# An earlier second and third operand and a sum made by VectorE in the seven-product matrix multiplication of a transformer block

## The chip, the cores and the metric

The kernel runs on one core of one Trainium2 chip. The time is that of one execution on the device, in microseconds (us), and lower is better. The engines are named as the profile names them: PE is TensorE, which multiplies matrices (PEld is its loading of weights), DVE is VectorE, ACT is ScalarE, POOL is GpSimd, SP is SyncE, which here only issues transfers. DMA transfers are issued by SP, and by POOL where they add to what the destination holds.

## The reference

A block of two attention branches and an MLP is followed by two layers of a second kind. The change touches the MLP of the first block only. With x of 512 tokens by 1024 and D_FF = 4096:

```python
h2 = rms_norm(x, norm_mlp[l])
x = x + jnp.square(jax.nn.relu(h2 @ w_up[l])) @ w_down[l]
```

All arithmetic is in float32. The kernel keeps that precision by splitting each operand into a high part and a low part and by running three passes (high by high, high by low, low by high) over them.

## The kernel before

The MLP is cut into four chunks of 1024 columns of D_FF. In each chunk PE first makes eight tiles of h2 @ w_up (the up products, `up_product`, 24 matmuls each), and then multiplies the squared result (the state) by a 1024 x 1024 block of w_down. In the first three chunks (`FAST` = 3) this second multiplication is done by two-by-two blocks in seven products in place of eight, `fast_product(c, n)` with n from 0 to 6. I call them P0 to P6. Each is 48 matmuls, in two halves b = 0 and 1 that go to two banks. P0 and P1 write tiles named G in the profile, P2, P3 and P6 tiles named T, P4 and P5 tiles named S.

**Weight operands.** Each product has a weight operand of 128 x 2048 elements (1 MB), made of the blocks (row half q, column half p) of w_down in the chunk. They lie in four buffers, called a and c (the two halves of K.raw), f (K.down_f) and e (K.down_e). In the order of the products the buffers are f, a, c, a, c, f, e. A block is loaded by SP (`down_block`), and a second one is added onto it in one of three ways:

- by an adding transfer of 1 MB that POOL issues, line 1138 in `block_added`: P0's operand f (semaphore f_sum), P1's operand a (a_sum), P5's operand f (f_sum again) and P4's operand c (c_sum);
- by DVE, line 1987, which writes e - c into a for P3 (semaphore w_made);
- not at all: P2 takes c and P6 takes e as loaded.

**Splitting.** Each operand then passes through two steps before PE can use it: `down_hi(c, n)`, line 1458, ACT writes the high part into the slab `K.w[:, j % 2]`, and `down_lo(c, n)`, line 1951, DVE writes the low part (raw minus high) and raises w_lo. PE waits for w_lo in `slab_ready`. There are two slabs, so the high part of P1 waits until the eighth up product has ended (tile_full), and that of a later product n until P(n-2) has ended (prod).

**The state.** The eight up tiles come in four pairs i = 0 to 3. For each tile k DVE takes the rectified value (`rectified`, line 1930), ACT squares it into `K.stage` (line 1474, h_sq), POOL makes four combinations of each pair (`state_combined(c, i)`, lines 1128 to 1133, h_comb), and ACT and DVE split the pieces: `state_hi` (line 1434) and `state_lo` (line 1937) for the plain ones, `state_hi_rest` and `state_lo_rest` for one turned piece and three combined ones. P2 is the first product that reads combined pieces of pair 3.

**Results.** `product_in(c, n, b)`, lines 1964 and 1966, adds a finished half of a product into x on DVE.

Each engine executes its own program in the order in which it is written, and a wait holds everything behind it on that engine. Thus the order of `state_combined` and `block_added` on POOL sets when each adding transfer starts, the order in `fast_chunk` of ACT sets when each high part starts, and that of DVE when each low part starts. SP loads block (0, 1) into f as soon as P0's low part is done.

Of the kernel before, what the change touches and what calls it, by code (L numbers as in the profile page):

```python
# [15 lines left out]
ALU = mybir.AluOpType  # L16
# [6 lines left out]
KT = D // P  # L23
# [65 lines left out]
READS = 2 * sum(len(to) for to in LANDS)  # L89
PLAIN_LO, TURNED_LO, MIXED_LO, STATE_LOS = (1, 2, 5, 8), (3, 6, 9, 11), (4, 7, 10, 12), 12  # L90
DOWN_SLABS = tuple(J_MLP + FAST_SLABS * c + HALF + n for c in range(FAST) for n in range(PRODUCTS))
# [101 lines left out]
def allocate(nc, ctx, K):  # L193
# [188 lines left out]
    K.a_sum = semaphore("a_sum")  # L382
    K.c_sum = semaphore("c_sum")
    K.w_made = semaphore("w_made")
# [585 lines left out]
def program_pool(nc, pool, K):  # L970
# [170 lines left out]
    for c in range(FAST):  # L1141
        state_combined(c, 0)
        pool.wait_ge(K.f_in, 64 * c + 32)
        block_added(c, 1, 0, K.down_f[:, :], K.f_sum)
        state_combined(c, 1)
        pool.wait_ge(K.a_in, 32 * (c + 1))
        block_added(c, 1, 1, down_raw(K, c, 1), K.a_sum)
        state_combined(c, 2)
        state_combined(c, 3)
        pool.wait_ge(K.f_in, 64 * (c + 1))  # L1150
        block_added(c, 0, 0, K.down_f[:, :], K.f_sum)
        pool.wait_ge(K.w_lo, down_slab(c, 2) + 1 + QA_MORE)
        pool.wait_ge(K.w_made, c + 1)
        block_added(c, 0, 1, down_raw(K, c, 4), K.c_sum)

# [55 lines left out]
def program_act(nc, act, K):  # L1211
# [231 lines left out]
    def down_hi(c, n):  # L1443


        if n < 2:
            act.wait_ge(K.tile_full, F_MLP + KT * c + 6 + 2 * n)
        else:
            act.wait_ge(K.prod, 2 * (PRODUCTS * c + n - 1))
        if n in (0, 5):  # L1450
            act.wait_ge(K.f_sum, 32 * c + (32 if n else 16))
        elif n in (1, 4):
            act.wait_ge(K.c_sum if n == 4 else K.a_sum, 16 * (c + 1))
        elif n == 3:
            act.wait_ge(K.w_made, c + 1)
        else:
            act.wait_ge(K.c_in if n == 2 else K.e_in, 32 * (c + 1))
        nc.scalar.activation(K.w[:, down_slab(c, n) % 2, 0, :], down_raw(K, c, n), ACT.Copy).then_inc(K.w_hi, 1)  # L1458

    def fast_chunk(c):  # L1460
        f = F_MLP + KT * c
        for i in range(4):
            if i == 0 and c:
                act.wait_ge(K.prod, 2 * PRODUCTS * c)
            if i < 3:
                split(Num(up_slab(c, i + 1)), Num(f + 2 * i))
            else:
                down_hi(c, 0)
            for k in range(2 * i, 2 * i + 2):
                act.wait_ge(K.tile_out, G_MLP + KT * c + k + 1)  # L1470
                if k % 2 == 0 and HALF * c + i >= 2:
# [4 lines left out]
                if k % 2 == 0:  # L1476
                    act.wait_ge(K.h_sq, KT * c + k + 1)
                    state_hi(c, i, B11, B12 + 1)
                    if i:
                        state_hi_rest(c, i - 1)  # L1480
        down_hi(c, 1)
        state_hi_rest(c, 3)
        for n in range(2, PRODUCTS):
            down_hi(c, n)
# [148 lines left out]
def program_vector(nc, dve, K):  # L1633
# [335 lines left out]
    def fast_chunk(c):  # L1969
        for i in range(4):  # L1970
            for k in range(2 * i, 2 * i + 2):
# [3 lines left out]
                if k % 2 == 0:  # L1975
                    state_lo(c, i, B11, B12 + 1, PLAIN_LO[i])
                    if i:
                        state_lo_rest(c, i - 1)
            if i < 2:
                split(Num(up_slab(c, i + 2)))  # L1980
# [7 lines left out]
        product_in(c, 0, 0)  # L1988
        for n in range(1, PRODUCTS):
            if n == 1:  # L1990
                down_lo(c, 2)
                state_lo_rest(c, 3)
            product_in(c, n - 1, 1)
            if 1 < n < PRODUCTS - 1:
                down_lo(c, n + 1)
            if n == PRODUCTS - 1:
                split(Num(up_slab(c + 1, 0)))
            product_in(c, n, 0)
        product_in(c, PRODUCTS - 1, 1)
        split(Num(up_slab(c + 1, 1)))  # L2000
# [836 lines left out]
```

## Time and profile before

| | |
|---|---|
| median of three runs | 1456.66 us (1454.26 to 1458.71) |
| profiled execution | 1456.53 us |
| its span in the trace | 1454.7 us |
| PE busy | 1434.6 us, 99% of the span |
| DVE, ACT, POOL busy | 58%, 44%, 30% |
| mean granted clock of PE | 0.997 of full speed |
| the three chunks with seven products | about 378 to 631 us |

The median lies 0.13 us above the profiled execution, whose time is 1.8 us above its span. A row of the timeline shows the start and the length of an instruction, or of a run of like ones; in brackets stands the time that the engine was idle ahead of it and what ended that. Instructions that issue DMA show the time of the issue only, and the landing has a view of its own. The rows themselves stand in the last section ahead of the prediction.

### The profile page before, as it was taken

What the parts mean: (1) busy time and instruction counts of PE and PEld (TensorE: products, weight loads), DVE (VectorE), ACT (ScalarE), POOL (GpSimd) and SP (SyncE); (2) the same over time, 40 slices, a digit from 0 to 9 for tenths busy, and PEclk for the clock granted to TensorE, in tenths of its full rate; (3) what the DMA queues carried; (4) which work ended last, traced back from release to release, by engine and by line L of the source; (5) the groups of instructions that cost most, each with busy time, mean ns of one, the idle gap of its engine ahead of it and who ended that gap; (6) DMA issues with size and microseconds to landing.
All of it is one profiled execution on the core that took longest, in us unless ns stands there. A gap on an engine that the chain in (4) does not pass through costs nothing.

```text
span 1454.7 us, 19451 instructions
## 1 busy us (share of the span) xinstructions
PE 1434.6 (99%) x7493; PEld 1219.8 (84%) x7493; DVE 841.0 (58%) x1354; ACT 638.6 (44%) x981; POOL 431.8 (30%) x421
## 2 busy tenths in 40 slices
PE   9999999999999999999999999999999999999999
PEld 7888888888888898988888888888888888888887
DVE  5648864444565665754478795444446879543432
ACT  5436862234343434334434695343333469533221
POOL 3004521011330504200406885121120678510000
PEclk9999999999999999999999999999999999999999
DMA  5564332324474675722232123222323212322232
GB/s 197 84 126 115 108 108 92 113 87 148 115 171 146 146 181 145 169 95 87 73 111 71 30 59 113 91 87 91 112 73 110 72 30 59 111 92 87 87 103 71
DMA packets 163788, 151.51 MB, mean 104 GB/s; under 512 B 36136, under 2 KB 141872, under 8 KB 163696
## 3 DMA queue, kind: packets, MB, share of 16 engines
q1 hardware_dynamic: 157200, 137.61, 31.7%
q0 software_dynamic: 6336, 12.58, 5.1%
q8 instruction: 60, 0.98, 0.3%
q14 instruction: 32, 0.26, 0.1%
q10 hardware_dynamic: 160, 0.07, 0.0%
HBM read 139.96 MB, written 2.92 MB: 98 GB/s over the span
## 4 chain that ended last, share of the span: by engine, by line
PE 86%; DVE 5%; ACT 3%; issue 2%; DMA 2%; POOL 2%; DVEq 0%; ACTq 0%; POOLq 0%
PE G L2273 61%; PE G L2255 3%; PE G L2731 3%; PE S L2255 3%; PE T L2364 3%; PE S L2566 2%; DMA raw<-in_w_down 2%; PE G L2388 2%; PE G L2395 2%; PE G L2485 1%; PE T L2566 1%; DVE w L1951 1%; ACT w L1458 1%; DVE sq L1778 1%; ACT w L1223 1%
## 5 line engine op out<-in xcount | busy, mean ns | idle before, releaser
L2273 PE MATMUL G<-gx,w 128*128 128x512 f32 x2928 | 672.3, 390 | 1.3 <-DVE w L1641 1.3
L2273 PEld LDWEIGHTS G<-gx,w 128*128 128x128 f32 x2928 | 548.5, 188 | 116.6 <-DVE w L1641 1.9
L1641 DVE TENSOR_TENSOR w<-raw,w 128x2048 fp32r<-128x2048 f32 (+3 forms) x97 | 221.8, 2286 | 206.5 <-ACT w L1223 206.3
L1223 ACT ACTIVATE w<-raw 128x2048 fp32r<-128x2048 f32 (+2 forms) x99 | 183.0, 1849 | 64.0 <-PE G L2731 14.9
L989 POOL TENSOR_TENSOR t<-t,rden 128x512 f32<-128x512 f32 (+2 forms) x128 | 108.8, 852 | 114.0 <-DVE rden L1784 112.1
L1031 POOL TENSOR_TENSOR t<-sig 128x512 f32<-128x512 f32 x24 | 35.4, 1474 | 338.1 <-DVE sig L1852 338.1
L1285 ACT ACTIVATE t<-sq,nm 128x512 f32<-128x512 f32 (+3 forms) x128 | 80.1, 626 | 17.1 <-DVE nm L1778 16.5
L2273 PE MATMUL G<-kvb,w 128*128 128x512 f32 x384 | 87.4, 389 | 0.0
L2273 PEld LDWEIGHTS G<-kvb,w 128*128 128x128 f32 x384 | 72.1, 188 | 15.0
L1679 DVE SCALAR_TENSOR_TENSOR sig<-G,rstd 128x512 f32<-128x512 f32 x48 | 32.8, 686 | 78.4 <-PE G L2273 78.4
L2364 PE MATMUL T<-ident,t 128*128 128x128 f32 x400 | 66.5, 277 | 3.4 <-POOL t L989 2.4
L1341 ACT ACTIVATE sig<-sig,lp 128x512 f32<-128x512 f32 x32 | 23.2, 724 | 103.0 <-DVE sig L1679 103.0
L2364 PEld LDWEIGHTS T<-ident,t 128*128 128x128 f32 x400 | 47.0, 140 | 22.5 <-POOL t L989 15.6
L2255 PE MATMUL S<-ab 96*128 96x512 f32 x192 | 56.8, 407 | 0.0
L1852 DVE TENSOR_TENSOR sig<-G,sig 128x512 f32<-128x512 f32 x48 | 32.0, 687 | 40.9 <-PE G L2273 40.9
L980 POOL TENSOR_TENSOR sumsq<-sumsq,sq 128x512 f32<-128x512 f32 x21 | 28.6, 1362 | 87.7 <-ACT sq L1241 69.5
L1799 DVE TENSOR_TENSOR pt<-T,pt 128x256 fp32r<-128x256 f32 (+2 forms) x96 | 50.6, 528 | 6.4 <-ACT pt L1329 3.2
L2566 PE MATMUL T<-hc,w 128*128 128x256 f32 x432 | 53.4, 284 | 0.3
L2566 PEld LDWEIGHTS T<-hc,w 128*128 128x128 f32 x432 | 52.3, 192 | 0.7 <-DVE hc L1937 0.7
L1778 DVE CUSTOM_DVE_ANT_0 sq<-S,zeros,hr 128x512 f32<-128x512 f32 x64 | 47.4, 743 | 5.7 <-PE S L2255 4.7
L1128 POOL TENSOR_TENSOR stage<-stage 128x256 f32<-128x256 f32 x12 | 10.0, 834 | 130.7 <-ACT stage L1474 130.7
L1474 ACT ACTIVATE stage<-t 128x512 f32<-128x512 f32 x24 | 15.2, 632 | 75.5 <-DVE t L1930 75.5
(285 smaller groups left out, 2277.6 us busy)
## 6 DMA issues: line engine op xcount, KB each, us to landing
raw<-in_w_in SPq DMA_DIRECT2D x98, 512.0 KB, 7.2
raw<-in_w_up SPq DMA_DIRECT2D x32, 512.0 KB
raw<-in_w_out SPq DMA_DIRECT2D x24, 512.0 KB
raw<-in_w_down SPq DMA_DIRECT2D x20, 512.0 KB, 4.3
down_f<-in_w_down SPq DMA_DIRECT2D x12, 512.0 KB, 5.2
down_f<-in_w_down POOLq DMA_DIRECT2D x6, 1024.0 KB, 10.0
raw<-in_w_down POOLq DMA_DIRECT2D x6, 1024.0 KB, 9.1
raw<-in_w_attn_proj SPq DMA_DIRECT2D x8, 512.0 KB
```

Source lines behind the costliest of these rows:

```text
L989: nc.gpsimd.tensor_tensor(p, p, K.rden[:, n % 4:n % 4 + 1].broadcast_to([P, (hi - lo) * P]), ALU.mult).then_inc(K.probs_ok, 1)
L1031: nc.gpsimd.tensor_tensor(K.t[:, m, :], sig[:, m, :], sig[:, 2 + m, :], ALU.add).then_inc(K.mix_ok, 1)
L1223: nc.scalar.activation(high, cut(K.raw[:, j % 2, 0:n]), ACT.Copy).then_inc(K.w_hi, 1)
L1285: nc.scalar.activation(K.t[:, n % 3, 0:width], K.sq[:, n % 2, 0:width], ACT.Exp, bias=K.nm[:, n % 4:n % 4 + 1], scale=-1.0, accum_out=K.de ...
L1641: nc.vector.tensor_tensor(low, cut(K.raw[:, s, 0:n]), high.bitcast(F32), ALU.subtract).then_inc(K.w_lo, 1)
L1778: nc.vector.tensor_tensor_reduce(K.sq[:, n % 2, c], K.S[(S + n) % 2][:, 0:(b1 - b0) * P], bias, scale, first, ALU.add, ALU.min, K.nm[:, n ...
L1799: nc.vector.tensor_tensor(K.pt[A.at(n)][m % 2][:, 1, b0:b1, e, :], K.T[(U + n) % 2][:, 0:(b1 - b0) * P].rearrange("p (k c) -> p k c", c=P) ...
L2255: mm = nc.tensor.matmul(bank, lhs, rhs, start=(i == 0), stop=(i == len(pairs) - 1))
L2273: mm = nc.tensor.matmul(b[:, :], w(p, k), x(q, k), start=(k == i == 0), stop=(k == kts - 1 and i == len(PASSES) - 1))
L2364: mm = nc.tensor.transpose(K.T[(U + n) % 2][:, k * P:(k + 1) * P], K.t[:, n % 3, c:c + P], K.ident[:, :])
L2566: mm = nc.tensor.matmul(product_bank(K, n, b)[:, m % 2 * SEQ // 2:(m % 2 + 1) * SEQ // 2], w[:, p, k, m * P:(m + 1) * P], K.hc[:, q, k, OP ...
L2731: mm = nc.tensor.matmul(b[:, :], K.m2[:, q, half * HALF + k, t * P:(t + 1) * P], w[:, p, k, :], start=(half == k == p == q == 0), stop=(ha ...
```

## The change

In each of the three chunks:

- ACT makes the high part of P1's operand ahead of the square of the eighth tile, and that of P2's operand right behind this square. The rest of the state parts of pair i - 1 now goes ahead of the squares of pair i, and not behind the first of them. DVE has the matching order, and the counts `PLAIN_LO`, `TURNED_LO` and `MIXED_LO` say after how many parts each is there.
- POOL makes the combinations of pair 2 ahead of the adding transfer of P1's operand, not behind it.
- The adding transfer of P4's operand is gone. DVE adds block (0, 1), which lies in f, onto c (new line 2000 of the changed kernel). As f must keep this block until then, the adding transfer of P5's operand now waits for this sum (w_made at an even count), where it waited for the load of f alone.
- In DVE's program for the products, the second half of a result goes in ahead of the next operand's low part.

POOL's program from the combinations of pair 1 on in chunk 0, before, with the lines of the kernel. The transfer `raw<-in_w_down` is P1's sum:

```order
L1138 DMA down_f<-in_w_down 128x4x512 [waits f_in]
L1128 TENSOR_TENSOR stage<-stage 128x256 [waits h_sq]
L1129 TENSOR_TENSOR stage<-stage 128x256
L1131 TENSOR_TENSOR stage<-stage 128x256 [waits h_comb]
L1133 TENSOR_TENSOR stage<-stage 128x256 [waits h_comb]
L1138 DMA raw<-in_w_down 128x4x512 [waits a_in]
L1128 TENSOR_TENSOR stage<-stage 128x256 [waits h_sq]
L1129 TENSOR_TENSOR stage<-stage 128x256
L1131 TENSOR_TENSOR stage<-stage 128x256 [waits h_comb]
L1133 TENSOR_TENSOR stage<-stage 128x256 [waits h_comb]
```

And now, where each line number is one lower:

```order
L1137 DMA down_f<-in_w_down 128x4x512 [waits f_in]
L1127 TENSOR_TENSOR stage<-stage 128x256 [waits h_sq]
L1128 TENSOR_TENSOR stage<-stage 128x256
L1130 TENSOR_TENSOR stage<-stage 128x256 [waits h_comb]
L1132 TENSOR_TENSOR stage<-stage 128x256 [waits h_comb]
L1127 TENSOR_TENSOR stage<-stage 128x256 [waits h_sq]
L1128 TENSOR_TENSOR stage<-stage 128x256
L1130 TENSOR_TENSOR stage<-stage 128x256 [waits h_comb]
L1132 TENSOR_TENSOR stage<-stage 128x256 [waits h_comb]
L1137 DMA raw<-in_w_down 128x4x512 [waits a_in]
L1127 TENSOR_TENSOR stage<-stage 128x256 [waits h_sq]
L1128 TENSOR_TENSOR stage<-stage 128x256
```

P1's sum moved from ahead of the combinations of pair 2 to behind them, and of the two transfers that followed each other at the end one is left, which waits for w_made.

ACT's program in chunk 1, from the high part of P0 (`w<-down_f`) to that of P6 (`w<-down_e`), before:

```order
L1458 ACTIVATE w<-down_f 128x2048 [waits f_sum,tile_full]
L1474 ACTIVATE stage<-t 128x512 [waits h_lo,tile_out]
L1434 ACTIVATE hc<-stage 128x512 [waits prod,h_sq]
L1434 ACTIVATE hc<-stage 128x256 [waits prod,h_sq]
L1434 ACTIVATE hc<-stage 128x1024 [waits prod,h_comb]
L1474 ACTIVATE stage<-t 128x512 [waits tile_out]
L1458 ACTIVATE w<-raw 128x2048 [waits a_sum,tile_full]
L1434 ACTIVATE hc<-stage 128x256 [waits prod,h_sq]
L1434 ACTIVATE hc<-stage 128x1024 [waits prod,h_comb]
L1458 ACTIVATE w<-raw 128x2048 [waits c_in,prod]
L1458 ACTIVATE w<-raw 128x2048 [waits w_made,prod]
L1458 ACTIVATE w<-raw 128x2048 [waits c_sum,prod]
```

And now, where line 1458 is line 1454 and line 1434 is line 1430:

```order
L1454 ACTIVATE w<-down_f 128x2048 [waits f_sum,tile_full]
L1430 ACTIVATE hc<-stage 128x256 [waits prod,h_sq]
L1430 ACTIVATE hc<-stage 128x1024 [waits prod,h_comb]
L1474 ACTIVATE stage<-t 128x512 [waits h_lo,tile_out]
L1430 ACTIVATE hc<-stage 128x512 [waits prod,h_sq]
L1454 ACTIVATE w<-raw 128x2048 [waits a_sum,tile_full]
L1474 ACTIVATE stage<-t 128x512 [waits tile_out]
L1454 ACTIVATE w<-raw 128x2048 [waits c_in,prod]
L1430 ACTIVATE hc<-stage 128x256 [waits prod,h_sq]
L1430 ACTIVATE hc<-stage 128x1024 [waits prod,h_comb]
L1454 ACTIVATE w<-raw 128x2048 [waits w_made,prod] x2
L1454 ACTIVATE w<-down_f 128x2048 [waits f_sum,prod]
```

The first `w<-raw`, which is P1's high part and waits for a_sum, moved from behind the last square (line 1474) to ahead of it, and P2's (which waits for c_in) from behind the last two state parts to ahead of them.

DVE's program in chunk 1, from the low part of P1, before (1987 makes e - c, 1964 takes a result in):

```order
L1951 TENSOR_TENSOR w<-raw,w 128x2048 [waits w_hi]
L1987 TENSOR_TENSOR raw<-down_e,raw 128x2048 [waits w_lo,c_in,e_in]
L1964 TENSOR_TENSOR x<-G,x 128x2x256 [waits prod_in,prod]
L1951 TENSOR_TENSOR w<-raw,w 128x2048 [waits w_hi]
L1942 SCALAR_TENSOR_TENSOR hc<-stage,hc 128x256 [waits h_hi]
L1937 TENSOR_TENSOR hc<-stage,hc 128x1024 [waits h_hi]
L1964 TENSOR_TENSOR x<-G,x 128x2x256 [waits prod_in,prod] x3
L1951 TENSOR_TENSOR w<-raw,w 128x2048 [waits w_hi]
L1964 TENSOR_TENSOR x<-T,x 128x2x256 [waits prod_in,prod] x2
```

And now, where line 1951 is line 1949, line 1987 line 1985 and line 1964 line 1962:

```order
L1949 TENSOR_TENSOR w<-raw,w 128x2048 [waits w_hi]
L1985 TENSOR_TENSOR raw<-down_e,raw 128x2048 [waits w_lo,c_in,e_in]
L1962 TENSOR_TENSOR x<-G,x 128x2x256 [waits prod_in,prod] x2
L1949 TENSOR_TENSOR w<-raw,w 128x2048 [waits w_hi]
L1940 SCALAR_TENSOR_TENSOR hc<-stage,hc 128x256 [waits h_hi]
L1935 TENSOR_TENSOR hc<-stage,hc 128x1024 [waits h_hi]
L1962 TENSOR_TENSOR x<-G,x 128x2x256 [waits prod_in,prod]
L2000 TENSOR_TENSOR raw<-raw,down_f 128x2048 [waits w_made,w_lo,f_in]
L1962 TENSOR_TENSOR x<-G,x 128x2x256 [waits prod_in,prod]
L1949 TENSOR_TENSOR w<-raw,w 128x2048 [waits w_hi]
```

Between the low parts of P2 and P3 stands the new sum of line 2000, with a result ahead of it and one behind it; one more result moved ahead of P2's low part.

The diff:

```diff
--- before.py
+++ after.py
@@ -87,7 +87,7 @@
 STARTS = (True, True, True, False, True, False, False)
 LANDS = (((1, 0, 1),), ((1, 1, 1),), ((1, 1, 1),), ((0, 1, -1),), ((0, 0, -1),), ((0, 1, 1),), ((1, 0, -1), (0, 0, 1)))
 READS = 2 * sum(len(to) for to in LANDS)
-PLAIN_LO, TURNED_LO, MIXED_LO, STATE_LOS = (1, 2, 5, 8), (3, 6, 9, 11), (4, 7, 10, 12), 12
+PLAIN_LO, TURNED_LO, MIXED_LO, STATE_LOS = (1, 4, 7, 10), (2, 5, 8, 11), (3, 6, 9, 12), 12
 DOWN_SLABS = tuple(J_MLP + FAST_SLABS * c + HALF + n for c in range(FAST) for n in range(PRODUCTS))
 G_LAST = G_L + (LAYERS - 1) * GL + 100
 
@@ -380,7 +380,6 @@
     K.a_in = semaphore("a_in")
     K.f_sum = semaphore("f_sum")
     K.a_sum = semaphore("a_sum")
-    K.c_sum = semaphore("c_sum")
     K.w_made = semaphore("w_made")
     K.prod = semaphore("prod")
     K.prod_in = semaphore("prod_in")
@@ -1143,15 +1142,12 @@
         pool.wait_ge(K.f_in, 64 * c + 32)
         block_added(c, 1, 0, K.down_f[:, :], K.f_sum)
         state_combined(c, 1)
+        state_combined(c, 2)
         pool.wait_ge(K.a_in, 32 * (c + 1))
         block_added(c, 1, 1, down_raw(K, c, 1), K.a_sum)
-        state_combined(c, 2)
         state_combined(c, 3)
-        pool.wait_ge(K.f_in, 64 * (c + 1))
+        pool.wait_ge(K.w_made, 2 * (c + 1))
         block_added(c, 0, 0, K.down_f[:, :], K.f_sum)
-        pool.wait_ge(K.w_lo, down_slab(c, 2) + 1 + QA_MORE)
-        pool.wait_ge(K.w_made, c + 1)
-        block_added(c, 0, 1, down_raw(K, c, 4), K.c_sum)
 
     for k in range(1, KT):
         for i, (total, square) in enumerate(((K.sumsq_f, K.sq_f), (K.sumsq, K.sq))):
@@ -1450,9 +1446,9 @@
         if n in (0, 5):
             act.wait_ge(K.f_sum, 32 * c + (32 if n else 16))
         elif n in (1, 4):
-            act.wait_ge(K.c_sum if n == 4 else K.a_sum, 16 * (c + 1))
+            act.wait_ge(K.w_made if n == 4 else K.a_sum, 2 * (c + 1) if n == 4 else 16 * (c + 1))
         elif n == 3:
-            act.wait_ge(K.w_made, c + 1)
+            act.wait_ge(K.w_made, 2 * c + 1)
         else:
             act.wait_ge(K.c_in if n == 2 else K.e_in, 32 * (c + 1))
         nc.scalar.activation(K.w[:, down_slab(c, n) % 2, 0, :], down_raw(K, c, n), ACT.Copy).then_inc(K.w_hi, 1)
@@ -1466,7 +1462,11 @@
                 split(Num(up_slab(c, i + 1)), Num(f + 2 * i))
             else:
                 down_hi(c, 0)
+            if i:
+                state_hi_rest(c, i - 1)
             for k in range(2 * i, 2 * i + 2):
+                if k == KT - 1:
+                    down_hi(c, 1)
                 act.wait_ge(K.tile_out, G_MLP + KT * c + k + 1)
                 if k % 2 == 0 and HALF * c + i >= 2:
                     act.wait_ge(K.h_lo, STATE_LOS * (c - (i < 2)) + MIXED_LO[(i + 2) % 4])
@@ -1476,11 +1476,9 @@
                 if k % 2 == 0:
                     act.wait_ge(K.h_sq, KT * c + k + 1)
                     state_hi(c, i, B11, B12 + 1)
-                    if i:
-                        state_hi_rest(c, i - 1)
-        down_hi(c, 1)
+        down_hi(c, 2)
         state_hi_rest(c, 3)
-        for n in range(2, PRODUCTS):
+        for n in range(3, PRODUCTS):
             down_hi(c, n)
         act.wait_ge(K.prod, 2 * (PRODUCTS * c + 6))
         split(Num(up_slab(c + 1, 0)), Num(0))
@@ -1973,9 +1971,9 @@
                     dve.wait_ge(K.h_sq, KT * c + k - 2)
                 rectified(k, Num(G_MLP + KT * c + k), Num(F_MLP + KT * c + k))
                 if k % 2 == 0:
-                    state_lo(c, i, B11, B12 + 1, PLAIN_LO[i])
                     if i:
                         state_lo_rest(c, i - 1)
+                    state_lo(c, i, B11, B12 + 1, PLAIN_LO[i])
             if i < 2:
                 split(Num(up_slab(c, i + 2)))
             if i == 2:
@@ -1987,15 +1985,19 @@
         nc.vector.tensor_tensor(down_raw(K, c, 3), K.down_e[:, :], down_raw(K, c, 2), ALU.subtract).then_inc(K.w_made, 1)
         product_in(c, 0, 0)
         for n in range(1, PRODUCTS):
+            product_in(c, n - 1, 1)
+            if n < PRODUCTS - 1:
+                down_lo(c, n + 1)
+            else:
+                split(Num(up_slab(c + 1, 0)))
             if n == 1:
-                down_lo(c, 2)
                 state_lo_rest(c, 3)
-            product_in(c, n - 1, 1)
-            if 1 < n < PRODUCTS - 1:
-                down_lo(c, n + 1)
-            if n == PRODUCTS - 1:
-                split(Num(up_slab(c + 1, 0)))
             product_in(c, n, 0)
+            if n == 1:
+                dve.wait_ge(K.f_in, 64 * (c + 1))
+                dve.wait_ge(K.w_lo, down_slab(c, 2) + 1 + QA_MORE)
+                dve.wait_ge(K.w_made, 2 * c + 1)
+                nc.vector.tensor_tensor(down_raw(K, c, 4), down_raw(K, c, 4), K.down_f[:, :], ALU.add).then_inc(K.w_made, 1)
         product_in(c, PRODUCTS - 1, 1)
         split(Num(up_slab(c + 1, 1)))
 
```

## Rows read from the trace of the kernel before

**Rows 1.** The page, part 1: busy time, share of span, instructions of each engine.

```profile
PE 1434.6 (99%) x7493; PEld 1219.8 (84%) x7493; DVE 841.0 (58%) x1354; ACT 638.6 (44%) x981; POOL 431.8 (30%) x421
```

**Rows 2.** Timeline of PE, chunk 0: start us, us, engine, line, tiles [idle before].

```profile
419.50 7.51 PE L2566 MATMUL G<-hc,w 128*128 128x256 f32 x48 [1.88 <-DVE w L1951]
```

**Rows 3.** Timeline of PE, from 440 us, the products of chunks 1 and 2.

```profile
500.36 12.05 PE L2566 MATMUL G<-hc,w 128*128 128x256 f32 x96
527.03 11.78 PE L2566 MATMUL S<-hc,w 128*128 128x256 f32 x96 [2.66 <-DVE w L1951]
...
587.95 12.05 PE L2566 MATMUL G<-hc,w 128*128 128x256 f32 x96
...
613.22 11.77 PE L2566 MATMUL S<-hc,w 128*128 128x256 f32 x96 [1.25 <-DVE w L1951]
```

**Rows 4.** Timeline of all engines, chunk 0.

```profile
406.02 3.35 DVE L1951 TENSOR_TENSOR w<-down_f,w 128x2048 fp32r<-128x2048 f32 x1 [2.51 <-ACT w L1458]
...
419.58 2.60 DVE L1987 TENSOR_TENSOR raw<-down_e,raw 128x2048 f32<-128x2048 f32 x1
419.98 1.29 POOL L1138 DMA_DIRECT2D down_f<-in_w_down  x1
...
439.43 10.82 PE L2566 MATMUL S<-hc,w 128*128 128x256 f32 x88 [0.91 <-DVE w L1951]
```

**Rows 5.** Timeline of all engines, chunk 1.

```profile
473.74 11.77 SPq L878 DMA_DIRECT2D raw<-in_w_down  x4
474.25 1.29 POOL L1138 DMA_DIRECT2D down_f<-in_w_down  x1
...
490.25 1.29 POOL L1138 DMA_DIRECT2D raw<-in_w_down  x1 [5.05 <-DMA raw<-in_w_down]
490.47 0.63 ACT L1474 ACTIVATE stage<-t 128x512 f32<-128x512 f32 x1 [2.69 <-DVE t L1930]
...
492.95 2.91 DVE L1951 TENSOR_TENSOR w<-down_f,w 128x2048 fp32r<-128x2048 f32 x1 [2.51 <-ACT w L1458]
493.78 2.68 POOL L1133 TENSOR_TENSOR stage<-stage 128x256 f32<-128x256 f32 x1
...
495.88 0.98 SPq L878 DMA_DIRECT2D down_f<-in_w_down  x2
...
522.73 1.91 ACT L1458 ACTIVATE w<-raw 128x2048 fp32r<-128x2048 f32 x1 [8.37 <-DMA raw<-in_w_down]
```

**Rows 6.** Timeline of all engines, chunk 2.

```profile
580.54 2.79 DVE L1951 TENSOR_TENSOR w<-down_f,w 128x2048 fp32r<-128x2048 f32 x1 [2.51 <-ACT w L1458]
```

**Rows 7.** Line 1138, landing: first transfer of each chunk, the one at 419.98, all twelve.

```profile
DMA to landing us min/median/max: 10.9/10.9/10.9
...
DMA to landing us min/median/max: 10.6/10.6/10.6
...
DMA to landing us min/median/max: 11.0/11.0/11.0
...
DMA to landing us min/median/max: 8.4/8.4/8.4
...
DMA to landing us min/median/max: 8.4/9.4/11.0
```

**Rows 8.** Groups of instructions by line, 500 to 528 us: count, busy us, mean ns, idle before.

```profile
L1951 DVE TENSOR_TENSOR w<-raw,w 128x2048 fp32r<-128x2048 f32 x4 | 9.4, 2347 | 8.0 <-ACT w L1458 8.0
L1458 ACT ACTIVATE w<-raw 128x2048 fp32r<-128x2048 f32 x4 | 7.6, 1907 | 11.0 <-DMA raw<-in_w_down 8.4 <-PE G L2566 2.6
L1964 DVE TENSOR_TENSOR x<-G,x 128x512 f32<-128x512 f32 x4 | 2.6, 681 | 0.0
L1937 DVE TENSOR_TENSOR hc<-stage,hc 128x1024 fp32r<-128x1024 f32 x2 | 2.4, 1222 | 0.2 <-ACT hc L1434 0.2
```

**Rows 9.** Groups by line and shape, 411 to 640 us: same columns.

```profile
L1133 POOL TENSOR_TENSOR stage<-stage 128x256 f32<-128x256 f32 x9 | 24.0, 2668 | 0.7
```

**Rows 10.** Stretches of 2 us, chunk 0: length, busy us of PE and others, PEclk.

```profile
420.00:422.00 2.00, 2.00 (x11) 2.00 (x11) 2.00 (x1) 1.93 (x2) 1.27 (x2) 0.50 0.04 2
```


## The prediction

> **What bounds the kernel now.** The page's first part comes first: PE is busy for 1434.6 of 1454.7 us [rows 1], so the end moves only if PE idles more or less, or computes at a lower clock. The change touches three stretches, the products of chunks 0 to 2, so I read PE's timeline there next. Chunk 0 has 1.88 us of idle time ahead of P1, whose 48 matmuls then take 7.51 us [rows 2], and 0.91 us ahead of P4 [rows 4]. In chunks 1 and 2 P0 and P1 follow each other (12.05 us for 96), and only P4 is late, by 2.66 and 1.25 us [rows 3]. That is 6.7 us of idle time, all of it ended by DVE's low part (L1951). A product takes some 5.8 to 5.9 us at full clock (11.78 for the two of the S tiles [rows 3]), so P1 of chunk 0 lost another 1.6 us: the row of 420 to 422 us shows a granted clock of 0.50, the lower of the two levels, 1.2 of 2.4 GHz, right after the idle stretch [rows 10]. All that the change can win is thus about 8.3 us.
>
> Then the timeline of all engines, for what the low part waited for. ACT sat idle for 8.37 us ahead of P4's high part, until the adding transfer of P4's operand landed [rows 5]. This is the wait that the change attacks. The views of the landing follow, since the change leaves three such transfers, and moves one.
>
> **What is removed.** P4's transfer, with its wait. If it alone went, 4.8 us of idle time ahead of P4 could go.
>
> **P1's sum moves behind four POOL operations.** In chunk 1 POOL issued it at 490.25, ahead of the combinations of pair 2 [rows 5]. Now these come first. They need the square of the sixth tile, which ended at 490.47 + 0.63 = 491.1 [rows 5]. Their fourth operation (L1133) took 2.68 us and ended at 496.46, and P0's low part on DVE, which started at 492.95, ended at 495.86 [rows 5]: POOL finished 0.6 us after DVE, and all nine of these have a mean of 2.67 us [rows 9]. I take it that it was held by DVE's operation. So the transfer can be issued 0.6 us after P0's low part ends. That part took 2.91 us beside the issue of the transfer, which is now gone from there, and the like operation has a mean of 2.35 [rows 8]; I take 2.5. From the starts of 406.02, 492.95 and 580.54 [rows 4 to 6] this gives issues at 409.1, 496.05 and 583.65. The bound on the other side: if POOL isn't held, four operations of 0.7 us end at 494.1 in chunk 1, 2 us earlier.
>
> **How long it then takes.** SP loads the next block into f right when P0's low part ends (495.88, [rows 5]), so both run together. The nearest rows are the first sums of the chunks: POOL issued that of chunk 1 at 474.25, half a microsecond after SP's loads at 473.74 [rows 5], and they landed after 10.9, 10.6 and 11.0 us. The shortest of all twelve took 8.4 [rows 7]. I take 10.8, with 8.4 as the other end. The sum then lands at 419.9, 506.85 and 594.45. P1's high part takes 1.91 [rows 8], so it ends at T = 421.8, 508.75 and 596.35. It cannot be covered: P0 ends at 417.6 in chunk 0 (419.50 less 1.88), and near 506.2 and 593.8 in the others (5.8 us after 500.36 and 587.95, [rows 2, 3]). PE waits.
>
> **What is queued behind it.** On ACT the last square, P2's high part and the last state parts stand behind this wait. POOL's combinations of pair 3 wait for the square, and DVE's program goes from T as follows (us after T; durations from [rows 8], the sum e - c takes 2.60 by [rows 4]):
>
> - P1's low part to 2.4, so P1 runs from 2.4 to 8.2
> - e - c to 5.0, two results of P0 to 6.35, P2's low part to 8.65: P2 starts 0.45 after P1 ends
> - the low parts of pair 3 to 10.2 (1.22 the longer). P2 reads them 1.1 us after its start, at 9.75, and waits some 0.5: P2 ends at 14.95. The combinations on POOL have until about 8 for this; they start at 0.7 and are four short operations, in part held by DVE
> - one result to 10.8, the new sum to 13.4 (not in the trace; at 2.60, as e - c has the same shape and also two inputs; no less than the 2.35 of a low part), a result to 14.0, P3's low part to 16.35: P3 starts 1.4 after P2 ends, and ends at 22.15
> - two results, then P4's low part to 19.9. Its high part has to wait for P2's end, 14.95, and is done at 16.9. P4 starts with no wait at 22.15.
>
> So P4 starts at 443.95, 530.9 and 618.5, against 439.43, 527.03 and 613.22 [rows 3, 4]: 4.5 + 3.9 + 5.3 = 13.7 us later. If the clock falls once more in P1, it takes 7.4 and ends at 9.8; P2 then ends at 15.6, still ahead of P3's low part. That cost lies in gaps already counted.
>
> **P5's sum.** It was issued early and had cover; now it is issued at 13.4, when f is free. With 10.6 us (between the twelve rows' median of 9.4 and 11.0, as SP's next slab starts 3 us behind it) it lands at 24.05, high and low part end at 28.25, and P4 ends at 27.95: 0.3 us in each chunk, 0.9 in all. At 8.4 it costs nothing, at 11.0 it costs 0.7 each. P6's operand has no new wait.
>
> **The rest** is costed at nothing. The state parts of earlier pairs go at most 1.1 us later (a high part waits for POOL), beside up products whose rectified values wait for PE anyway. In chunk 0 the last plain part is done near 412.2, and P0 asks for it near 412.9; without this cover it would cost the difference.
>
> **The sum.** 13.7 + 0.9 = 14.6 us on the profiled execution's 1456.53, which is within 0.13 of the median: 1471.1 us, 1.0% slower. A measurement of this kernel tells about 0.3%, or 4.4 us, from no change.
>
> A rule speaks for still more. The row shows that POOL's transfer at 419.98 was issued with DVE's e - c in progress (419.58 for 2.60 us), and it landed after 8.4 us, the shortest of all [rows 4, 7]. The Trainium skill (SBUF — State Buffer, section "SBUF: two separate sides") says that POOL can't write the descriptors of its transfers while DVE holds the port pair that they share, which it ties to DVE's two-port modes. This trace disagrees for DVE's operation with two inputs, and the forecast goes by the trace.
>
> **The rivals.**
>
> - *The sum of P1 isn't late* (7%). If it lands by the end of the up products, T is 1.9 us after P0's start: 413.7, 502.3 and 589.9. P4 would then start at T + 22.15, 3.6, 2.6 and 1.2 us earlier than before, less 0.9 for P5: 1450.0 us. Against it: issue to landing would have to be about 3 to 4.5 us. The point from which this decides: T must come about 4.9 us earlier than forecast, on average, a landing in under 6 us, for no change.
> - *The quick end* (10%). A landing in 8.4 us takes 2.4 from each T: 7.2 less, 1463.9. If POOL isn't held either, another 2 each: 1458, no change that can be told. For it: P1's sums might share the engines more kindly than the first ones did. Against it: both run from the same instant.
> - *The clock stays low* (7%). The idle stretches ahead of P1 are now 6.6, 5.0 and 5.0 us. If P1 runs wholly at the lower level it takes 11.6, and P4 starts 3.5 later in each chunk: 1481.6. Against it: after 1.88 us of idle time only some 3 us were at the lower level, and 2.66 us in chunk 1 did nothing to the 11.78 of the next two products [rows 3, 10].
> - *DVE holds up POOL's transfer of P5* (4%), by a low part of 2.3 us behind the new sum. Then each P5 waits 2.3 more: 1478. Against it: the 8.4 us of [rows 7]. The rule cited above would lead here.
>
> **The numbers.** My forecast, 72%, covers 1464 to 1477: the lower end is 8.4 us of landing, the upper one takes in a DVE slowed by POOL (P0's low part took 3.35 in chunk 0, [rows 4], 1.0 over the mean) at two long operations of each chunk, 6 us. The range of 1461 to 1479 leaves out the first and the third rival and the fastest third of the second. Slower by over 0.3%: 72 + 6 + 7 + 4 = 89%; within: 4%; faster: 7%.
>
> **What the profile will show.** If I am right, L1137 issues the transfer into raw near 496 in chunk 1; ACT's L1454 waits some 8 us for it; the last square starts near 509, behind P1's high part; PE has idle time of 5 to 7 us ahead of P1 and some 1.4 ahead of P3 in each chunk, and none ahead of P4. P4's wait on a DMA is gone. I am wrong if P1's high part starts with the end of the up products, or if the transfer is issued ahead of P0's low part's end.

## The result: slower, and the profile after

The changed kernel took 1471.22 us (median of four runs, 1470.97 to 1473.55), the kernel before 1456.45 us (four runs, 1454.26 to 1458.71). The ratio is 1.0105, with a 95% interval of 1.0086 to 1.0123: slower by 1.0%. (The ratio is estimated from all runs, so here and below it need not be exactly that of the two medians.) The profiled execution took 1471.01 us, with a span of 1469.2.

The page of the changed kernel, part 1, answers to [rows 1]:

```profile
PE 1436.1 (98%) x7493; PEld 1222.0 (83%) x7493; DVE 848.3 (58%) x1357; ACT 638.8 (43%) x981; POOL 438.4 (30%) x418
```

PE is busy 1.5 us longer and the span is 14.5 us longer, so nearly all of the loss is idle time of PE. Where it lies is in its timeline, here chunk 1 of the changed kernel, which answers to [rows 3] (start us, us, engine, line, tiles, in brackets the idle time ahead and what ended it):

```profile
502.82 5.91 PE L2568 MATMUL G<-hc,w 128*128 128x256 f32 x48
513.92 7.33 PE L2568 MATMUL G<-hc,w 128*128 128x256 f32 x48 [5.19 <-DVE w L1949]
521.09 1.24 PE L2568 MATMUL T<-hc,w 128*128 128x256 f32 x9
523.04 4.94 PE L2568 MATMUL T<-hc,w 128*128 128x256 f32 x39 [0.71 <-DVE hc L1935]
529.34 5.98 PE L2568 MATMUL T<-hc,w 128*128 128x256 f32 x48 [1.36 <-DVE x L1962]
535.15 11.68 PE L2568 MATMUL S<-hc,w 128*128 128x256 f32 x96
```

P4 starts with no wait, at 535.15, as the change was to bring about. But there is a new idle stretch of 5.19 us ahead of P1, one of 0.71 inside P2 and one of 1.36 ahead of P3. The waits of PE from 400 us on, summed over the three chunks, of the kernel before and then of the changed kernel (what waited, for what: us in total, times, longest):

```profile
PE S L2566 <- DVE w L1951: 4.8, 3, 2.7
PE G L2566 <- DVE w L1951: 1.9, 1, 1.9
```

```profile
PE G L2568 <- DVE w L1949: 15.5, 3, 5.4
PE T L2568 <- DVE x L1962: 3.8, 3, 1.4
PE T L2568 <- DVE hc L1935: 1.0, 2, 0.7
```

The change removed waits of 4.8 us (the S tiles, P4) and 1.9 us and put 20.3 us in their place. The timeline of the other engines in chunk 1 shows the cause; it answers to [rows 5]:

```profile
495.41 2.52 DVE L1949 TENSOR_TENSOR w<-down_f,w 128x2048 fp32r<-128x2048 f32 x1 [2.51 <-ACT w L1454]
495.87 2.67 POOL L1132 TENSOR_TENSOR stage<-stage 128x256 f32<-128x256 f32 x1
...
497.96 0.88 SPq L877 DMA_DIRECT2D down_f<-in_w_down  x2
...
498.48 1.28 POOL L1137 DMA_DIRECT2D raw<-in_w_down  x1
...
509.63 1.91 ACT L1454 ACTIVATE w<-raw 128x2048 fp32r<-128x2048 f32 x1 [8.82 <-DMA raw<-in_w_down]
511.45 0.61 ACT L1474 ACTIVATE stage<-t 128x512 f32<-128x512 f32 x1
```

POOL issues P1's sum at 498.48, 0.55 us after DVE's low part of P0 has ended and behind the fourth combination. SP's loads went out at 497.96. The transfer lands after 11.1 us, and ACT has waited 8.82 us for it; the last square comes behind. To compare executions whose start differs, I count from the start of P0 to that of P6. Over the three chunks that is 114.5 us before and 131.5 after: 17.0 us more.

### The profile page after: what moved, and what is told of

Read it like the earlier page. It is cut to its first block, busy times and chain, and to the rows that moved or that the text cites. A ratio compares the mean times of both kernels' runs of the same rounds, so it can differ in the third digit from the quotient of the medians.

```text
span 1469.2 us, 19451 instructions
## 1 busy us (share of the span) xinstructions
PE 1436.1 (98%) x7493; PEld 1222.0 (83%) x7493; DVE 848.3 (58%) x1357; ACT 638.8 (43%) x981; POOL 438.4 (30%) x418
## 4 chain that ended last, share of the span: by engine, by line
PE 84%; POOL 4%; DVE 4%; issue 2%; DMA 2%; ACT 2%; DVEq 0%; ACTq 0%; POOLq 0%
PE G L2275 59%; PE G L2257 3%; PE G L2733 3%; PE S L2257 3%; PE T L2366 2%; PE T L2568 2%; PE S L2568 2%; DMA raw<-in_w_down 2%; PE G L2390 2%; PE G L2397 2%; POOL stage L1132 1%; PE G L2487 1%; POOL stage L1128 1%; DVE sq L1776 1%; PE G L2697 1%
## 5 line engine op out<-in xcount | busy, mean ns | idle before, releaser
L1219 ACT ACTIVATE w<-raw 128x2048 fp32r<-128x2048 f32 (+2 forms) x99 | 183.0, 1849 | 63.8 <-PE G L2733 14.9
L1281 ACT ACTIVATE t<-sq,nm 128x512 f32<-128x512 f32 (+3 forms) x128 | 80.2, 626 | 16.9 <-DVE nm L1776 16.3
L1127 POOL TENSOR_TENSOR stage<-stage 128x256 f32<-128x256 f32 x12 | 13.5, 1128 | 156.1 <-ACT stage L1474 156.1
L2568 PE MATMUL G<-hc,w 128*128 128x256 f32 x288 | 41.4, 311 | 15.5 <-DVE w L1949 15.5
L2568 PEld LDWEIGHTS G<-hc,w 128*128 128x128 f32 x288 | 40.7, 220 | 16.3 <-DVE w L1949 16.1
```

Source lines behind the costliest of these rows:

```text
L1219: nc.scalar.activation(high, cut(K.raw[:, j % 2, 0:n]), ACT.Copy).then_inc(K.w_hi, 1)
L1281: nc.scalar.activation(K.t[:, n % 3, 0:width], K.sq[:, n % 2, 0:width], ACT.Exp, bias=K.nm[:, n % 4:n % 4 + 1], scale=-1.0, accum_out=K.de ...
L2568: mm = nc.tensor.matmul(product_bank(K, n, b)[:, m % 2 * SEQ // 2:(m % 2 + 1) * SEQ // 2], w[:, p, k, m * P:(m + 1) * P], K.hc[:, q, k, OP ...
```

## Experiments

In the table, "chunks" is the time from P0's start to P6's start, summed over the three chunks in the profiled execution. The medians are compared with those of the kernel before on the same chip. They vary from set to set (1454.42 to 1456.45 us for the kernel before), so kernels of different sets are better compared by their ratios and chunks.

| kernel | median us | before us | ratio (95%) | chunks us |
|---|---|---|---|---|
| before | | | | 114.5 |
| changed | 1471.22 | 1456.45 | 1.0105 (1.0086 to 1.0123) | 131.5 |
| x1_pool_back | 1454.31 | 1454.42 | 0.9992 (0.9980 to 1.0004) | 112.8 |
| x2_pool_alone | 1468.33 | 1454.42 | 1.0098 (1.0081 to 1.0115) | 127.7 |
| x3_sum_alone | 1457.80 | 1454.42 | 1.0016 (1.0006 to 1.0027) | 116.2 |
| x4_high_back | 1467.78 | 1454.42 | 1.0088 (1.0073 to 1.0103) | 126.0 |
| x5_load_waits | 1465.61 | 1456.17 | 1.0064 (1.0046 to 1.0081) | 124.7 |
| x7_sum_later | 1487.46 | 1456.17 | 1.0213 (1.0198 to 1.0228) | 145.3 |
| x6_two_sums | 1451.82 | 1456.17 | 0.9967 (0.9957 to 0.9978) | 109.4 |
| x9_two_sums_before | 1453.82 | 1456.17 | 0.9981 (0.9972 to 0.9990) | 112.7 |
| x8_difference_later | 1449.37 | 1454.74 | 0.9960 (0.9946 to 0.9974) | 107.8 |
| x6_again | 1450.81 | 1454.74 | 0.9968 (0.9957 to 0.9980) | 109.3 |

**x1_pool_back: undo the place on POOL.** In the changed kernel:

```diff
         state_combined(c, 1)
-        state_combined(c, 2)
         pool.wait_ge(K.a_in, 32 * (c + 1))
         block_added(c, 1, 1, down_raw(K, c, 1), K.a_sum)
+        state_combined(c, 2)
         state_combined(c, 3)
```

> The changed kernel with one thing undone: POOL issues the adding transfer of P1's operand ahead of the combinations of pair 2 again. If the place of this transfer is the cause, P1's high part waits for no transfer, P1 follows P0 with no gap, only some 1.7 us of waiting is left ahead of P3, and P4 starts some 25 us after P0 and not 32.3: about 1453 us. If the loss lies in what is queued behind the high part on ACT, or in the new sum on DVE, it stays near 1471.

It took 1454.31 us, 0.1 below the kernel before. The timeline of x1 in chunk 1:

```profile
488.77 1.29 POOL L1137 DMA_DIRECT2D raw<-in_w_down  x1 [4.99 <-DMA raw<-in_w_down]
...
499.14 1.92 ACT L1454 ACTIVATE w<-raw 128x2048 fp32r<-128x2048 f32 x1 [1.89 <-PE G L2275]
```

The transfer goes out 10.2 us ahead of P0 (498.94) and not 4.3, and ACT waits for PE's last up product and for no transfer. (In chunk 0 ACT still waits 0.98 us for it, without a gap between P0 and P1.) PE's idle time from 400 us on is now all ahead of and inside the T products:

```profile
PE T L2568 <- DVE x L1962: 4.1, 3, 1.4
PE T L2568 <- DVE hc L1935: 3.4, 3, 1.6
```

So the place of one transfer accounts for the whole 15.5 us ahead of P1. The rest of the change is worth nothing measurable in the median (the chunks are 1.7 us shorter than before): it wins the waits ahead of P4 and P1 and gives most of them back inside P2 and ahead of P3. The wait inside P2 I had not expected. With it P4 starts 26.8, 25.8 and 25.8 us after P0, where I had put 25.

**x2_pool_alone: the place on POOL, and nothing else.** In the kernel before:

```diff
         state_combined(c, 1)
+        state_combined(c, 2)
         pool.wait_ge(K.a_in, 32 * (c + 1))
         block_added(c, 1, 1, down_raw(K, c, 1), K.a_sum)
-        state_combined(c, 2)
         state_combined(c, 3)
```

> The kernel before with one thing changed: POOL issues the adding transfer of P1's operand behind the combinations of pair 2. If that is the cause, P1 starts some 5 us late in each chunk and P4 follows 5 to 6 us later than before: about 1472 us. If the transfer is hidden in this order, about 1457.

It took 13.9 us longer than the kernel before. The expected 1472 us would have been 17.6 more than this chip's 1454.4. PE's timeline of x2 shows the wait ahead of P1, and of 2.66 us ahead of P4 in chunk 1 only 0.28 are left:

```profile
513.86 7.37 PE L2566 MATMUL G<-hc,w 128*128 128x256 f32 x48 [4.85 <-DVE w L1951]
521.06 11.68 PE L2566 MATMUL T<-hc,w 128*128 128x256 f32 x96
533.02 11.78 PE L2566 MATMUL S<-hc,w 128*128 128x256 f32 x96 [0.28 <-DVE w L1951]
```

The order on POOL thus costs by itself nearly what the whole change costs. Counted from P0, P4 starts 5.2, 3.2 and 4.9 us later than before and not 5 to 6: behind a late P1 the old waits ahead of P4 (0.91, 2.66 and 1.25 us) are covered, all but those 0.28 us.

**x3_sum_alone: DVE's sum, and nothing else.** In the kernel before, POOL's fourth transfer goes out and the addition goes in. The count of w_made that P3's and P4's high parts wait for changes as in the change under study.

```diff
-        pool.wait_ge(K.f_in, 64 * (c + 1))
+        pool.wait_ge(K.w_made, 2 * (c + 1))
         block_added(c, 0, 0, K.down_f[:, :], K.f_sum)
-        pool.wait_ge(K.w_lo, down_slab(c, 2) + 1 + QA_MORE)
-        pool.wait_ge(K.w_made, c + 1)
-        block_added(c, 0, 1, down_raw(K, c, 4), K.c_sum)
...
             product_in(c, n, 0)
+            if n == 1:
+                dve.wait_ge(K.f_in, 64 * (c + 1))
+                dve.wait_ge(K.w_lo, down_slab(c, 2) + 1 + QA_MORE)
+                dve.wait_ge(K.w_made, 2 * c + 1)
+                nc.vector.tensor_tensor(down_raw(K, c, 4), down_raw(K, c, 4), K.down_f[:, :], ALU.add).then_inc(K.w_made, 1)
```

> The kernel before with one thing changed: DVE makes P4's operand (an addition behind the first result of P1), three adding transfers in a chunk. My theory: the wait for the transfer ahead of P4 goes, but P3's low part comes 2.3 us later and PE waits ahead of P3; P4 starts 26.3 us after P0, against 27.7, 26.7 and 25.3 before: 1457 to 1458 us. The rival that the new sum is what costs 4 to 5 us in each chunk gives 1470.

It took 1457.80 us, 0.2% above the kernel before and within the expected 1457 to 1458; the rival of 1470 us fell. P4 starts 28.1, 26.0 and 27.5 us after P0, where I had put 26.3: chunk 0 still has its wait ahead of P1 (2.16 us), and in chunk 2 P3 ran at a lower clock after its wait (7.49 us for 48 matmuls). PE's timeline of x3, P3 in the chunks 0 to 2:

```profile
431.34 5.98 PE L2567 MATMUL T<-hc,w 128*128 128x256 f32 x48 [0.90 <-DVE x L1960]
...
518.19 5.99 PE L2567 MATMUL T<-hc,w 128*128 128x256 f32 x48 [1.95 <-DVE x L1960]
...
605.04 7.49 PE L2567 MATMUL T<-hc,w 128*128 128x256 f32 x48 [1.95 <-DVE x L1960]
```

The wait for the transfer ahead of P4 became a wait for DVE ahead of P3. P3 waits for a result (line 1960), not for its low part: it writes the T banks that P2 wrote, and DVE takes P2's first half out of them only behind P3's low part, which the new sum has delayed.

**x4_high_back: P1's high part behind the last square again.** In the changed kernel:

```diff
             for k in range(2 * i, 2 * i + 2):
-                if k == KT - 1:
-                    down_hi(c, 1)
                 act.wait_ge(K.tile_out, G_MLP + KT * c + k + 1)
...
+        down_hi(c, 1)
         down_hi(c, 2)
         state_hi_rest(c, 3)
```

> The changed kernel with one thing undone: ACT makes P1's high part behind the square of the eighth tile. P1's sum still lands as late, so P1 starts as late, but the square and POOL's combinations of pair 3 are no longer held: the wait inside P2 goes and P3 comes about 1 us earlier in each chunk: about 1468 us. If the square held behind the high part is the whole loss, 1457.

It took 1467.78 us. Against the changed kernel the chunks are 5.5 us shorter: P1 is as late as there (idle 5.36, 5.01 and 4.79 us), but the waits inside P2 are gone and of the 3.8 us ahead of P3 0.5 is left. What stood behind the high part on ACT was a third of the loss at most (5.5 of 17.0 us of the chunks; by the medians, each against the kernel before on its own chip, only 13.4 us in place of 14.8), and the late sum is the rest. The two do not simply add up: x1, with the high part early and the sum early too, has no loss.

**x5_load_waits: SP's load behind the sum.** In the changed kernel:

```diff
         sp.wait_ge(K.w_lo, down_slab(c, 0) + 1 + QA_MORE)
+        sp.wait_ge(K.a_sum, 16 * (c + 1))
         down_block(c, 0, 1, K.down_f[:, :], K.f_in)
```

> The changed kernel, but SP loads the next block into f only when P1's sum has landed, so that the two don't run together. If the load slows the adding transfer, this lands after some 8.9 us and not 11.1, P1 starts 2.2 us earlier in each chunk, and the time is about 1465 us. If it doesn't, the landing stays at 11 us and the time at 1471.

It took 1465.61 us, as expected. In chunk 1 POOL issues the sum at 496.44 and SP, who waits for its landing, issues its load at 505.08: 8.6 us and not 11.1.

```profile
496.44 1.27 POOL L1138 DMA_DIRECT2D raw<-in_w_down  x1
...
505.08 0.88 SPq L877 DMA_DIRECT2D down_f<-in_w_down  x2
```

Running together with SP's load of 1 MB costs the adding transfer of 1 MB 2.5 us here (11.1 against 8.6; in the chunks 0 and 2 it lands after 9.5 and 8.3 us and not 11.2 and 10.8), and this passes on to P1 (idle 2.69 us in place of 5.19).

**x7_sum_later: the new sum behind P3's low part.** In the changed kernel:

```diff
             product_in(c, n, 0)
-            if n == 1:
+            if n == 2:
                 dve.wait_ge(K.f_in, 64 * (c + 1))
```

> The changed kernel, but DVE makes the new sum behind P3's low part and the first result of P2, not ahead of them. P3's gap of 1.4 us goes, P4 starts some 1.3 us earlier after P1; the transfer of P5's operand is issued 4.5 us later and has no cover left, so PE waits some 3 us ahead of P5: about 1475 us. If P5's transfer still has cover, 1467.

It took 1487.46 us. The mechanism held and its size didn't. P3's wait is gone, but P5's sum is issued at 536.25 in chunk 1, and its high part waits 7.46 us for it. From the timeline of x7:

```profile
536.25 1.29 POOL L1137 DMA_DIRECT2D down_f<-in_w_down  x1 [8.85 <-DVE raw L2000]
...
545.42 1.91 ACT L1454 ACTIVATE w<-down_f 128x2048 fp32r<-128x2048 f32 x1 [7.46 <-DMA down_f<-in_w_down]
...
550.41 8.22 PE L2568 MATMUL S<-hc,w 128*128 128x256 f32 x48 [4.05 <-DVE x L1964]
```

P5 waits 4.05 us and then takes 8.22 for 48 matmuls: about another 2.4 us of lower clock (granted 0.50 from 550 to 554 us), which here, unlike in P1, has no later wait to disappear in. Both together are 6.4 us in this chunk (5.5 and 5.2 in the others: waits of 3.84 and 3.80, then 7.50 and 7.24 us), where I had put 3.

**x6_two_sums: P1's sum early, P4's and P5's made by DVE.** In the kernel of x1, the sum for P4 goes behind P3's low part as in x7, POOL's transfer into f goes out, the counts of w_made change with it, and:

```diff
             product_in(c, n - 1, 1)
+            if n == 3:
+                dve.wait_ge(K.w_made, 3 * c + 2)
+                nc.vector.tensor_tensor(K.down_f[:, :], K.down_f[:, :], K.down_e[:, :], ALU.add).then_inc(K.w_made, 1)
             if n < PRODUCTS - 1:
```

> The changed kernel with the transfer of P1's operand ahead of the combinations of pair 2 again, the new sum behind P3's low part, and P5's operand made by DVE too (block (0, 0) is in e, so f + e), one adding transfer less. P4 should start 24.3 to 25.3 us after P0, and P5 waits for no transfer: 1448 to 1452 us. If DVE becomes the bound of each product, P4 starts later than 26 us after P0 and nothing is won against the kernel before.

It took 1451.82 us, 0.3% below the kernel before. A second set of runs beside x8 gave 1450.81 (ratio 0.9968):

> The kernel of x6 once more, on the same chip as x8, for the comparison: 4 to 5 us below the kernel before, as in its first runs.

P4 starts 24.8 us after P0 in all three chunks. PE's waits from 400 us on:

```profile
PE T L2569 <- DVE hc L1933: 2.7, 3, 0.9
PE S L2569 <- DVE w L1947: 1.5, 3, 0.5
```

**x9_two_sums_before: the same two sums in the kernel before.** The edit is that of x3 with the sum at n == 2, and the second sum of x6, so that POOL's transfers for P4 and P5 are both gone.

> The kernel before with both sums, those of P4's and P5's operand, made by DVE behind P3's low part, and its old order on ACT and DVE elsewhere. P4 should start some 25.6 us after P0 in every chunk, against 27.7, 26.7 and 25.3 before: 1452 to 1454 us. If DVE becomes the bound, 1457 or more.

It took 1453.82 us, 0.2% below the kernel before. P4 starts 25.1 us after P0 in the chunks 1 and 2, but 27.6 in chunk 0, which I had missed. The chunks of x9 are 3.3 us longer than those of x6, and 2.8 of that lie in chunk 0: there x9 still has the wait ahead of P1 (idle 2.10, then 7.49 us for the 48 matmuls). P1's high part starts 3.5 us after P0 there, behind the last square (412.86 against 409.37), and 0.2 us after P0 in x6, which has no such wait. x6 and x9 differ in the rest of the order too, so that the early high part alone does it is argued.

**x8_difference_later: e - c behind P0's results.** In the kernel of x6:

```diff
-        dve.wait_ge(K.e_in, 32 * (c + 1))
-        dve.wait_ge(K.c_in, 32 * (c + 1))
-        dve.wait_ge(K.w_lo, down_slab(c, 1) + 1 + QA_MORE)
-        nc.vector.tensor_tensor(down_raw(K, c, 3), K.down_e[:, :], down_raw(K, c, 2), ALU.subtract).then_inc(K.w_made, 1)
         product_in(c, 0, 0)
         for n in range(1, PRODUCTS):
             product_in(c, n - 1, 1)
+            if n == 1:
+                dve.wait_ge(K.e_in, 32 * (c + 1))
+                dve.wait_ge(K.c_in, 32 * (c + 1))
+                dve.wait_ge(K.w_lo, down_slab(c, 1) + 1 + QA_MORE)
+                nc.vector.tensor_tensor(down_raw(K, c, 3), K.down_e[:, :], down_raw(K, c, 2), ALU.subtract).then_inc(K.w_made, 1)
```

> The kernel of x6, but DVE makes e - c behind the two results of P0 and not ahead of them. If POOL's combinations of pair 3 are late because DVE's additions from SBUF hold POOL (they took 2.3 and 2.8 us each instead of 0.74), they end earlier, the wait of 0.89 us inside P2 shrinks to 0.3 or less in each chunk, and the time is some 2 us below that of x6. If POOL is late for another reason, nothing changes.

It took 1449.37 us, 0.4% below the kernel before and 1.4 us below x6 on the same chip; the chunks are 1.5 us shorter. POOL's combinations of pair 3 and DVE's e - c, first in the changed kernel (chunk 1), then in x8. In x6 the four combinations take 2.33, 2.79, 0.74 and 2.67 us, much as in the changed kernel:

```profile
512.15 2.30 POOL L1127 TENSOR_TENSOR stage<-stage 128x256 f32<-128x256 f32 x1 [12.39 <-ACT stage L1474]
...
514.00 2.60 DVE L1985 TENSOR_TENSOR raw<-down_e,raw 128x2048 f32<-128x2048 f32 x1
514.42 2.77 POOL L1128 TENSOR_TENSOR stage<-stage 128x256 f32<-128x256 f32 x1
...
517.15 0.74 POOL L1130 TENSOR_TENSOR stage<-stage 128x256 f32<-128x256 f32 x1
...
517.97 2.67 POOL L1132 TENSOR_TENSOR stage<-stage 128x256 f32<-128x256 f32 x1
```

```profile
499.36 2.29 DVE L1947 TENSOR_TENSOR w<-raw,w 128x2048 fp32r<-128x2048 f32 x1 [1.19 <-ACT w L1452]
...
499.92 2.33 POOL L1127 TENSOR_TENSOR stage<-stage 128x256 f32<-128x256 f32 x1 [6.99 <-ACT stage L1472]
...
502.21 0.73 POOL L1128 TENSOR_TENSOR stage<-stage 128x256 f32<-128x256 f32 x1
502.90 0.74 POOL L1130 TENSOR_TENSOR stage<-stage 128x256 f32<-128x256 f32 x1
...
503.72 0.74 POOL L1132 TENSOR_TENSOR stage<-stage 128x256 f32<-128x256 f32 x1
503.77 2.83 DVE L1987 TENSOR_TENSOR raw<-down_e,raw 128x2048 f32<-128x2048 f32 x1
```

The first combination is still held, by P1's low part. With DVE on results, whose one input comes from a PSUM bank, the other three take 0.74 us each. The idle time inside P2 is gone from PE's waits; only P4's 0.5 us a chunk is left. Not all of the 0.89 us a chunk are won, as P2 and P3 together take 12.16 us and not the 11.68 of x2. This is the best version of the study.

## Why the prediction was right, point by point

**P1's sum, its place.** Shown. Put alone into the kernel before it costs 13.9 us (x2), and taken alone out of the changed kernel it gives 16.9 us back (1471.22 against 1454.31, on different chips; the chunks alone 18.7). The step by which DVE's low part holds POOL's fourth combination held: the issue came 4.3 us ahead of P0's start in chunks 1 and 2, as forecast. In chunk 0 it came 4.3 ahead too (405.15 against 409.43), where I had 2.6, for I had counted from the old start of P0's low part, which stood 5.7 us ahead of P0 there and now stands 7.3 ahead. The idle stretches ahead of P1 are 5.42, 5.19 and 4.88 us, where I had 6.6, 5.0 and 5.0.

**Its landing.** Forecast 10.8 us, measured 11.2, 11.1 and 10.8. That the load by SP at the same instant is the reason was argued from the first sums, and x5 shows it: 8.6 us without that load.

**What is queued behind.** The step that was mis-sized. From T, the end of P1's high part, I had P3 at 16.35 and P4 at 22.15. In chunk 1 (T = 511.5) P3 came at 17.8 and P4 at 23.6, 1.45 us later, and so they did in the other two chunks. The rows of DVE and POOL ahead of P3, chunk 1:

```profile
521.76 1.22 DVE L1935 TENSOR_TENSOR hc<-stage,hc 128x1024 fp32r<-128x1024 f32 x1 [0.84 <-ACT hc L1430]
...
523.51 2.28 DVE L2000 TENSOR_TENSOR raw<-raw,down_f 128x2048 f32<-128x2048 f32 x1
...
526.09 1.29 POOL L1137 DMA_DIRECT2D down_f<-in_w_down  x1 [5.45 <-DVE raw L2000]
526.31 2.28 DVE L1949 TENSOR_TENSOR w<-raw,w 128x2048 fp32r<-128x2048 f32 x1
...
528.51 1.28 DVE L1962 TENSOR_TENSOR x<-T,x 128x512 f32<-128x512 f32 x2
```

There are two parts. POOL's four combinations took until 520.64, 9.1 us after T and not some 8, since DVE's operations held three of them for 2.30, 2.77 and 2.67 us (the rows stand under x8): the wait inside P2 was 0.71, and DVE's two state parts ended 1.2 us later than I had put them. The new sum gave 0.3 of this back, with 2.28 us where I had 2.60, and P3's low part ended 0.7 late. And P3 needs P2's first result out of its bank, not only its own low part, some 0.7 us more: this wait of PE I had overlooked.

**P5's sum.** Forecast 0.3 us a chunk, measured none. The transfer took 9.0 us in chunk 1 and not 10.6. Its cover, from its issue to P4's end, was 14.9 us where I had 14.55: it was issued 1.15 us later after T than forecast, but P4 ended 1.45 later. x7 shows that the cover is thin: issued 3.4 to 3.9 us later after P1's start than in the changed kernel, it costs 5 to 6 us a chunk.

**The rest** was put at nothing, and PE had no idle time inside P0 in any chunk.

**The clock.** The row of 422 to 424 us of the changed kernel has the lower level (0.50) again, and P1 took 7.78, 7.33 and 8.55 us in the three chunks. It was to disappear in the waits behind P1, and did so: in the chunks 0 and 1 PE still waited for DVE's state parts inside P2 (0.26 and 0.71 us), and in chunk 2, with the slowest P1, ahead of P3 (1.10 us). So DVE and not PE set what followed, and P4 came 23.6 us after T in all three. In the row of 422 to 424 us the granted clock is the third number from the end:

```profile
422.00:424.00 2.00, 2.00 (x11) 2.00 (x11) 2.00 (x3) 0.00 (x0) 2.00 (x1) 0.50 0.00 0
```

**The sum.** Forecast 14.6 us, measured 14.8 between the medians. But the chunks alone grew by 17.0. Of the 2.4 us that the forecast lacks there, 4.35 are the 1.45 us behind T in each chunk; against them stand 0.8 for T, which came earlier after P0 than forecast (1.1 in chunk 0, against 0.3 later in chunk 1), 0.9 for P5's sum, and 0.3 between P4 and P6 (11.5 us a chunk, 11.6 before). The profiled execution of before started P0 at 411.71 and that of the changed kernel at 409.43. This difference of 2.3 us arose in the first 36 us of the program, which the change doesn't touch: like matmuls (line 2273 before, 2275 now) start at 38.10 and at 35.80. Over the profiles of this study P0's start in the first chunk stands either at 409.0 to 409.4 or at 411.4 to 412.0. The close hit of 0.1 us is in part luck: 2.4 us of missing cost in the chunks met 2.3 us of a start that varies. That the medians carry the same difference as these two profiles is likely and not shown, as the other executions left no trace.

**The rivals.** That P1's sum isn't late fell with the 8.82 us of ACT's wait. x1 is this rival's case and shows that its price was off: I had 1450.0, 6.5 us below the kernel before, and x1 stands 0.1 below. P4 comes 23.6 us after T there too, not 22.15. For the quick end, x5 gives its price: with 8.6 us the time is 1465.6, where I had 1464. That the clock stays low for all of P1 fell (8.55 us at most, not 11.6). That DVE holds up POOL's transfer fell too: P5's sum, issued at 526.09 with P3's low part on DVE from 526.31, landed after 9.0 us. The Trainium skill (SBUF — State Buffer, section "SBUF: two separate sides") says that an operation of DVE with two SBUF inputs excludes only an operation of POOL that reads SBUF. As I read it, issuing a transfer beside such an operation is then harmless, and the trace agrees, in this landing as in the held combinations of x8's comparison. The prediction took the 8.4 us of [rows 4, 7] for a disagreement. It was none: what that page says of the descriptors is said of DVE's two-port modes, and e - c has two inputs.

## What to carry to other kernels

An adding transfer's deadline is set where it is issued: count from its issue to its landing (here 8.3 to 11.6 us), and move nothing ahead of it on its queue without asking what work covers it. Moving a consumer earlier pays only where its producer is early: here P1's high part ahead of the last square made the chunks 5.5 us longer while its sum was late (the changed kernel against x4), and the chunks of x6, where the sum is early, are 3.3 us shorter than those of x9. Replacing a transfer by a sum on a compute engine removes its latency, but takes a slot in that engine's order; here the slot behind the next low part was the good one (x6 and x9), and a bad one while a transfer still depended on the sum (x7). Both sums with the first one in the early slot were not tried.

## What the runs showed of the hardware that was not expected

- An operation on POOL that reads SBUF takes 0.74 us beside DVE's reading of a PSUM bank, and 2.3 to 2.8 us when DVE combines two operands of 128 x 2048 from SBUF at that time; it then ended 0.6 us after DVE's (514.45 against 513.86 in the changed kernel).
- It goes both ways. DVE's e - c took 2.29 us in x2 and x4, where no combination of POOL ran at the time, 2.60 in the changed kernel, where one of POOL ended 0.45 us after its start, and 2.83 in x8, where one of 0.74 us had started 0.05 us ahead of it.
- The new sum of the same shape took 2.28 us in the changed kernel, with no combination of POOL beside it. The 2.60 us that the prediction took for it were those of e - c at 419.58 in the kernel before, where POOL's fourth combination ended at 420.04; without such a neighbour the two take the same time.
- After about 5 us of idle time (4.8 to 5.7) PE ran the next 48 matmuls in 7.3 to 8.7 us in place of 5.8; after 1.88 (before, chunk 0) and 2.69 us (x5, chunk 1) it took 7.51, after 2.38 (x5, chunk 2) 6.01, and after 2.66 (before, chunk 1) nothing was lost. Idle stretches of nearly the same length, 2.4 to 2.7 us, thus cost from 0 to 1.7 us.
